# Seven chunks of the second modulation set go from TensorE's products to a running sum on VectorE

## What is computed

```python
mod = jax.nn.silu(c) @ w_ada[l] + b_ada[l]
sh1, sc1, gt1, sh2, sc2, gt2 = jnp.split(mod[:, None, :], 6, axis=-1)
h = rms_norm(x, g_pre_mix[l]) * (1.0 + sc1) + sh1
...
mix = jnp.concatenate([o_diff, o_nat], axis=-1) @ w_out[l]
x = x + gt1 * rms_norm(mix, g_post_mix[l])
h2 = rms_norm(x, g_pre_ffn[l]) * (1.0 + sc2) + sh2
f = moe_ffn(h2, ...)
x = x + gt2 * rms_norm(f, g_post_ffn[l])
```

## Time and profile before

| what | us |
|---|---|
| median of 3 runs | 1941.0 (1939.54 to 1942.81) |
| profiled execution, own time | 1943.13 |
| its span, first to last instruction | 1940.8 |
| TensorE (PE) busy | 1879.4 (97%) |
| VectorE (DVE) busy | 667.3 (34%) |
| ScalarE (ACT) busy | 370.3 (19%) |
| mean granted TensorE clock | 0.998 of 2.4 GHz |

### The profile page before, as it was taken

How to read it: one execution, slowest core, us unless ns; L and a number is a source line. 1 busy time by engine, 2 the same in 40 slices (tenths; PEclk the granted TensorE clock), 3 DMA queues, 4 the chain that set the end, 5 groups by cost and what they waited for, 6 DMA issues and landing times.

```text
span 1940.8 us, 25687 instructions
## 1 busy us (share of the span) xinstructions
PE 1879.4 (97%) x9767; PEld 1135.4 (59%) x9768; DVE 667.3 (34%) x1289; ACT 370.3 (19%) x836; POOL 35.3 (2%) x57
## 2 busy tenths in 40 slices
PE   8999999999999999999989999999999999999998
PEld 6877544333334434443333336878887489988864
DVE  2451411011011111110110113354656557655564
ACT  2232211111011111110110103442111031321111
POOL 2200000000000000000000001000000000000000
PEclk9999999999999999999999999999999999999999
DMA  9959699999989979999999999324544452345430
GB/s 370 289 209 411 253 421 422 422 422 421 422 346 400 422 302 422 421 422 422 421 422 421 422 422 320 126 87 130 172 165 167 147 164 97 109 158 162 161 116 22
DMA packets 156542, 564.45 MB, mean 291 GB/s; under 512 B 10814, under 2 KB 94040, under 8 KB 101952
## 3 DMA queue, kind: packets, MB, share of 16 engines
q1 hardware_dynamic: 153312, 554.96, 73.8%
q0 software_dynamic: 2416, 7.87, 1.3%
q10 hardware_dynamic: 752, 0.75, 0.1%
HBM read 562.49 MB, written 1.05 MB: 290 GB/s over the span
## 4 chain that ended last, share of the span: by engine, by line
PE 79%; DMA 14%; SPq 4%; DVE 1%; issue 1%; ACT 1%; ACTq 0%; DVEq 0%
PE psum L1038 15%; DMA ring<-in_w_dram 14%; PE psum L1422 12%; PE psum L1066 9%; PE psum L1514 6%; PE psum L1214 5%; SPq L581 4%; PE psum L1566 4%; PE psum L793 3%; PE psum L860 3%; PE psum L1008 2%; PE psum L1025 2%; PE psum L1450 2%; PE psum L1626 2%; PE psum L1047 1%; PE psum L1592 1%
## 5 line engine op out<-in xcount | busy, mean ns | idle before, releaser
L1038 PE MATMUL psum<-ring,arena 128*64 128x512 f32 x2176 | 491.2, 596 | 38.8 <-DMA ring<-in_w_dram 38.8
L1038 PEld LDWEIGHTS psum<-ring,arena 128*64 128x64 f32 x2176 | 151.9, 137 | 369.5 <-issue 252.0
L2496 DVE TENSOR_SCALAR arena<-psum 128x512 f32<-128x512 f32 x34 | 23.5, 692 | 726.0 <-PE psum L1047 726.0
L1066 PE MATMUL psum<-ring,arena 128*64 128x512 f32 x1088 | 241.0, 595 | 3.2
L1066 PEld LDWEIGHTS psum<-ring,arena 128*64 128x64 f32 x1088 | 77.6, 137 | 145.1 <-issue 145.1
L1856 ACT ACTIVATE arena<-arena 128x512 f32<-128x512 f32 x34 | 21.4, 630 | 558.5 <-DVE arena L2496 558.5
L1422 PE MATMUL psum<-arena,mixT 128*128 128x256 f32 x528 | 120.9, 379 | 0.0
L1422 PEld LDWEIGHTS psum<-arena,mixT 128*128 128x128 f32 x528 | 98.8, 190 | 12.6
L1422 PE MATMUL psum<-ring,hT 128*128 128x256 f32 x352 | 83.5, 379 | 0.0
L1008 PE MATMUL psum<-arena 128*128 128x128 f32 x544 | 75.1, 281 | 0.0
L1008 PEld LDWEIGHTS psum<-arena 128*128 128x128 f32 x544 | 65.9, 191 | 11.7 <-issue 11.7
(11 more groups left out here) (521 smaller groups left out, 2256.1 us busy)
## 6 DMA issues: line engine op xcount, KB each, us to landing
ring<-in_w_dram SPq DMA_DIRECT2D x384, 1024.0 KB, 23.0
ring<-in_ffn_w_dram SPq DMA_DIRECT2D x66, 1024.0 KB, 5.4
ring<-in_w_ada_dram SPq DMA_DIRECT2D x16, 1024.0 KB, 10.5
ring<-in_odd_w_in_dram SPq DMA_DIRECT2D x16, 1024.0 KB, 5.5
ring<-in_even_w_in_dram SPq DMA_DIRECT2D x13, 1024.0 KB, 12.8
ring<-in_w_in_dram SPq DMA_DIRECT2D x12, 1024.0 KB, 36.5
ring<-in_ada_blocks_dram SPq DMA_DIRECT2D x8, 1024.0 KB, 17.3
ring<-in_w_out_dram SPq DMA_DIRECT2D x4, 1024.0 KB, 14.3
```

Source lines behind the costliest of these rows:

```text
L1038: mm = nc.tensor.matmul(bank[4 + q][64 * h:64 * h + 64, :], xg[:, k, SLOTS * r:SLOTS * (r + 1)], ring[(C_MOE + k) % RING][:, (2 * h + q) * ...
L1066: mm = nc.tensor.matmul(bank[7][64 * h:64 * h + 64, :], act_T[:, at:at + 64], w[:, k, 512 * h:512 * h + 512], start=(f == 0), stop=(f == 7))
```

## The change

Chunks m = 0 to 6 of the second set are no longer multiplied by TensorE. VectorE multiplies each by silu(c) of its rows and adds it to a running sum of 128 x 2048 (`added_rows`, arena columns 0 to 2047) in slots 13 (three of them), 17, 19 (two) and 21. TensorE adds the sum over the partitions into bank 7 with four matmuls against ones in slot 24 (`added_sum`), then takes chunk 7 in slot 24, 8 to 11 in slot 25, 12 to 15 in slot 26. `chunk_done` is raised by eight with chunk 7. The third set goes to bank 1. The load of `h_tok` waits for the sum to be read (`ada_summed`). `heads(7)` and `ada_columns(0)` move into `out_first`, behind its first seven eighths.

```diff
-ADA_B_PER_SLOT = N_ADA_B // WIN_TAIL
+ADA_ADDED_AT = (13, 13, 13, 17, 19, 19, 21)
+ADDED = len(ADA_ADDED_AT)
+ADA_AT = {WIN_SLOTS: (7,), WIN_SLOTS + 1: range(8, 12), WIN_SLOTS + 2: range(12, 16)}
...
+        added_rows = region(0, 2048)
...
-            pool.wait_ge(S.mix_saved, DIFF_HEADS)
+            pool.wait_ge(S.ada_summed, 1)
             pool.dma_start(h_tok, x[0].rearrange("(a p) d -> p a d", p=P)).then_inc(S.tok_loaded, 16)
...
+            def added_sum():
+
+                pe.wait_ge(S.ada_added, ADDED)
+                for g in range(4):
+                    mm = nc.tensor.matmul(bank[7][32 * g:32 * g + 32, :], ones[:, 0:32], added_rows[:, 512 * g:512 * g + 512],
+                                          start=True, stop=False)
+                mm.then_inc(S.ada_summed, 1)
+
+            def ada(m):
+
+                home = (bank[7], bank[1])[m // KT]
+                arrived(C_ADA_B + m)
+                w = ring[(C_ADA_B + m) % RING]
+                if m == KT:
+                    pe.wait_ge(S.proj_saved, N_WIN)
+                k = m % KT
                 for g in range(4):
                     mm = nc.tensor.matmul(home[32 * g:32 * g + 32, :], silu_c[:, k, :], w[:, 512 * g:512 * g + 512],
-                                          start=(k == 0), stop=(k == KT - 1))
-                mm.then_inc(S.chunk_done, 1)
+                                          start=(m == KT), stop=(k == KT - 1))
+                mm.then_inc(S.chunk_done, ADDED + 1 if m == ADDED else 1)
...
                 if slot < WIN_SLOTS:
                     win_half(slot // 2, slot % 2)
-                else:
-                    for n in range(ADA_B_PER_SLOT):
-                        ada(N_ADA_A + ADA_B_PER_SLOT * (slot - WIN_SLOTS) + n)
+                if slot == WIN_SLOTS:
+                    added_sum()
+                for m in ADA_AT.get(slot, ()):
+                    ada(m)
                 if slot in TURN_AT:
                     turn_attention(TURN_AT.index(slot))
-                if slot in HEADS_AT:
+                if slot in HEADS_AT[:-1]:
                     heads(HEADS_AT.index(slot))
...
-            ada_columns(0)
...
                 for n, some in enumerate((range(KT - 1), (KT - 1,))):
+                    if n == 1:
+                        heads(UNITS - 1)
+                        ada_columns(0)
                     pe.wait_ge(S.mix_saved, UNITS - 1 + n)
...
-                V.tensor_copy(ada_rows[n + 1], (bank[7], bank[3])[n]).then_inc(S.ada_saved, 1)
+                V.tensor_copy(ada_rows[n + 1], (bank[7], bank[1])[n]).then_inc(S.ada_saved, 1)
...
+            def add_block(m):
+
+                n = C_ADA_B + m
+                dve.wait_ge(landed[n % RING], 16 * (n // RING + 1))
+                w, factor = ring[n % RING], silu_c[:, m, 0:1]
+                if m == 0:
+                    dve.wait_ge(S.c_ready, 1)
+                    V.tensor_scalar(added_rows, w[:, :], factor, None, ALU.mult).then_inc(S.ada_added, 1)
+                else:
+                    dve.wait_ge(S.ada_added, m)
+                    V.scalar_tensor_tensor(out=added_rows, in0=w[:, :], scalar=factor, in1=added_rows,
+                                           op0=ALU.mult, op1=ALU.add).then_inc(S.ada_added, 1)
+
...
                 if slot in SUB_SCALE_AT:
                     sub_scale(SUB_SCALE_AT.index(slot))
+                for m in range(ADDED):
+                    if ADA_ADDED_AT[m] == slot:
+                        add_block(m)
```

More of the change, by code:

```diff
@@ L276, in shape_constants @@
     return early, late
-NAMES = """ada_saved ada_turned c_loaded c_turned alibi_loaded vec_loaded x_loaded early_loaded bias_loaded lam_loaded moe_loaded late_loaded cmp_loaded
+NAMES = """ada_saved ada_turned ada_added ada_summed c_loaded c_turned alibi_loaded vec_loaded x_loaded early_loaded bias_loaded lam_loaded moe_loaded late_loaded cmp_loaded
 ident_loaded vec_turned vec_saved c_cleared c_ready x_turned x_ready lam_dots lam_spread lam_exp bias_ready
```

## The result

The changed kernel takes 1944.6 us (median of 22 runs, 1941.94 to 1950.85), the kernel before beside it on the same chips 1941.7 (22 runs). The ratio is 1.0017, 95% interval 1.0010 to 1.0025: 3.3 us slower (1.9 to 4.9), where 2.6 were forecast; the medians differ by 2.9. TensorE has less to do and the kernel takes longer.

A forecast was written before the change was run, and what follows sets the result against it. TensorE and nearly tied DMA transfers were taken as bounds; with h_tok's 2.46 in the stream, w_out lands at 157.0, plus 9.02 ends out_first at 166.0 against 163.40: 1941.0 + 2.6 = 1943.6 us, range 1940.0 to 1947.2.

The forecast's parts named there:

- main case: Modulation chunks 12 to 15 and w_out paced by transfers at full clock: 2.6 us slower, 1943.6; chance 47%.
- The transfers end last, and the saving is given back to them: Ahead of out_first's end: TensorE has 5.4 us less to do but loses it waiting for transfers; end 166.0 against 163.40.
- h_tok's megabyte costs about what its bytes take: In the ring's stream from about 140 us: the load delays every chunk from 12 on by 2.46 us, bounds 0 to 3.6.
- The rival of a load that costs little: h_tok's packets fall into holes or w_out's first chunk loses its lag: out_first ends 162.4 to 164.5, 1940.0 to 1942.1; 14%.
- TensorE's own order: From 135.96 us to out_first's end, if only TensorE's sequence limited: 159.05, 4.35 less than 163.40.
- VectorE's steps are covered: Slots 13 to 21: seven products of 2.46, 17 us in all, fit idle stretches and cost nothing; one shift 0.35 late.
- A microsecond at out_first's end is one at the end of the kernel: The expert stage begins when TensorE gets there, so a microsecond at 163.40 carries through to the kernel's end.
- The first release costs nothing, w_out lands at 154.5 without other traffic: Chunk 12's slot frees at about 137.75 instead of 136.85, covered by chunk 11's transfer; w_out's first landing stays at 154.5.
- Waits of 1 to 1.6 at each of the last four chunks: Sign in the trace after: at line 722, chunks 12 to 15 each wait 1 to 1.6 us for the ring's transfer.
- The clock's fall, 1.7 to 3.4 with a chance of 30%: Rival: TensorE's clock drops in the transfer-paced stretch and out_first loses 1.7 to 3.4 us; 1945.3 to 1947.0, chance 30%.
- 2.0 of work that could have filled the wait has been moved behind it: heads(7) and ada_columns(0), formerly done ahead of the wait for w_out, now follow it: 2.0 us.
- The rival of the saving that arrives: Up to out_first's end only TensorE's order limits: 4.35 us less, 1936.7; needs chunks landing 8 us earlier; chance 7%.

The follow-up runs named there:

- the order undone: The changed kernel with heads(7) and ada_columns(0) put back ahead of out_first's first product; 1948.89 us, ratio 1.0045.
- one filler: The changed kernel with one idle product of 512 columns on TensorE behind each of chunks 12, 13 and 14; 1944.34 us, ratio 1.0013.
- the load moved alone: The kernel before with only h_tok's load moved, to wait for the last saved projection (about 137 us); 1943.57 us, ratio 1.0006.
- early slots: The changed kernel with slots of chunks 0 to 6 released by VectorE's count and SP's loads reordered; 1938.17 us, ratio 0.9983.

## Why the prediction was right

By the prediction's own signs the number is better borne out than its main case. That case was transfers at full clock; "a granted clock below 1.00 between 146 and 164" was to be wrong, and all three profiles of the changed kernel have it. out_first was to wait 1 to 2 us for w_out, and in none of the three did it: chunk 15's product and the turn, slowed by the lower clock, ended later than w_out's landing. The time fits because the fall cost 0.8 and not 1.7 to 3.4.

**Held.** The steps below, each with what was measured.

- *The transfers end last, and the saving is given back to them.* Chunks 13 to 15 wait 2.36, 1.43 and 0.55; removing the load of h_tok leaves the length of before (27.45 and 27.73 against 27.35), not 5.4 less.
- *h_tok's megabyte costs about what its bytes take.* I took 2.46 within 0 to 3.6. w_out's first chunk landed 2.3 later with the load in the stream than without (156.4 against 154.1), and 2.6 later in the kernel before. For chunk 15 it was more. Where chunk 15 had to be waited for, its product gives the landing: in six profiles with the load in the stream it starts 18.15 to 19.51 behind the first landmark (mean 18.80; the changed kernel thrice, the order undone, one filler, the load moved alone), in the two without it 15.85 and 16.12. The difference is 2.8; in the kernel before, the load moved alone put chunk 15 back by 3.7, past my upper bound. The rival of a load that costs little rested on holes in the stream, and a common set of engines, which I held against it, does not exclude those: the full stream, 420 to 425 GB/s, left none.
- *TensorE's own order.* Paper said 159.05 if nothing else paced it; with early slots it ended at 158.99. This carries the wait for VectorE (1.0 forecast, 0.94 measured) and the 9.02 of out_first (9.12 measured with one filler, 157.15 to 166.27).
- *VectorE's steps are covered.* 15.6 us against 17 forecast, the shift 0.02 late instead of 0.35. A sum of product and chunk over 2048 columns took 2.34 to 2.35, the first, a product alone, 1.28.
- *A microsecond at out_first's end is one at the end of the kernel.* From the start of the first expert's product to the span's end lie 1734.3 to 1736.1 us in the profiles without a fall of 6.8 us behind it (the three highest of these, 1735.1 to 1736.1, have one of 3.4 us near 1210), and 1737.7 to 1739.4 in those with one or two, wherever that stage starts between 198.5 and 208.4.

**The sizes that were off, all small.**

- *The first release costs nothing, w_out lands at 154.5 without other traffic.* It landed at 154.1, but by two errors that cancelled: chunk 15 came at 151.65 instead of 150.9, and the 1.1 of lag on w_out's first chunk was gone. The first of these is the later first release, which was to cost nothing: SP issued chunk 12 at 137.83 instead of 137.02, it landed at 144.2 instead of 143.4, and the 0.8 stayed to chunk 15. Why the chunk in flight did not cover it is open, since by 145 the engines had moved only 0.07 MB less. The lag's going was luck.
- *Waits of 1 to 1.6 at each of the last four chunks.* The load shares the engines with the ring for 7 us instead of pushing it aside at once. Chunk 12 was hardly late in the profile of the result (0.67 and 1.20 of waiting in the other two), chunk 13 took the brunt (3.4 from landing to landing where 2.46 is usual), and w_out's first chunk came at 156.44 where I had 157.0.
- *The clock's fall, 1.7 to 3.4 with a chance of 30%.* The mechanism came in every profile of the changed kernel, so 30% was low, and its price was high. What the end would be at full clock I can only work out: it is chunk 15's landing plus 2.48 for w_out plus 9.12: a length of 29.76, 29.75 and 30.83 in the three profiles, against 30.98, 29.76 and 31.90. The fall cost 1.2, 0 and 1.1, mean 0.8, because most of it lay inside waits for the ring, where it is free. The page of the Trainium skill that I weighed (TensorE: Matmul & The Clock Gate, Why this matters for your kernels), with its idle gaps longer than any of mine, spoke against this rival; the trace disagrees, for the gaps here were at most 2.4 us. The measurement decides.

Put together: the mean full-clock length of the three profiles is 30.1, 2.8 above before's 27.35; with the clock's 0.8 it is 3.5 above, and the runs say 3.3 (1.9 to 4.9). The forecast of 2.6 lacked the clock's share; the interval alone could not tell the two apart.

**The step that was wrong, without a price.** "2.0 of work that could have filled the wait has been moved behind it". It could not have filled it: heads(7) needs ScalarE's copy of a turn that itself ends late, and with the old order the stretch is longer, 32.11 against 29.76 to 31.90. Chunk 15 was 0.7 later there than the mean of the six, and about 1.0 is the order's own (w_out at 157.8 and 9.12 would give 166.9 instead of 167.90).

**What I did not see.** The rival of the saving that arrives had 7%, because "no row offers room" for landings 8 us earlier. In the changed kernel that is so; but the view of the stretch 98 to 136 had shown an idle stream in front of a saturated one, and the slots that VectorE had read were the room.

## What to carry to other kernels

Work taken off an engine that is tied with the transfers is worth at most the slack between the two; before making it faster, ask which loads the edit moves, and through which wait on the place that its scratch data takes. If another engine now reads the ring, let its count hand the slots back and order the loads by when slots come free: only with that did the removed products become worth 3 us here, where without it they cost 3. And in a kernel whose clock falls at changing places, compare landmarks of several profiles, since one span is some 3.5 us off by a single fall of 6.8 us.

## What the runs showed of the hardware

- The granted clock went from 2.4 to 1.2 GHz in the paced stretch in four of four profiles that had the seven chunks removed, the load of h_tok in the stream and no filler in the waits (2.4 us the longest of them), in the first of them after 3.42 us with 1.06 of work. In the kernel before with the load moved alone, whose one wait is 1.21, it stayed at 1.00. So it did without the load, with waits of 1.4 and 4.68 of 8.00 us busy:

```profile
146.00:154.00 8.00, 4.68 (x40) 1.33 (x32) 2.70 (x4) 1.91 (x8) 0.00 (x0) 1.00 1.01 424
```

That is the kernel with h_tok's load late; with one filler TensorE was busy 8.40 of 10.50 and the clock stayed too. What decides between them was not tried.

- The clock also fell for 6.8 us with TensorE busy throughout, at 223.4 in the kernel before, at 227.9 with the order undone, at 226.4 and again at 1216.2 with one filler, at 1214 and 1218 in two of the three profiles of the changed kernel, and at neither place in the third. One of them:

```profile
1214.00:1220.80 6.80, 6.80 (x74) 6.22 (x74) 0.00 (x0) 2.62 (x5) 0.00 (x0) 0.50 0.67 228
```

From the first expert's product to the span's end it is 1734.6 on average in the four profiles without any such fall, 1735.4 in the three with one of 3.4 us, 1738.2 in the four with one of 6.8 us and 1739.4 in the one with two: a fall of 6.8 us costs some 3.5. How much of the scatter from run to run this is was not measured.

- Two full queues did not share the engines' time evenly: 35% for GpSimd's, 65% for SP's. By packets they did, 268 against 274; GpSimd's carried 3.9 KB on average (1.04 MB) and SP's 7.3 (1.99 MB). The window of the profile with the order undone has 261 against 262. The same megabyte that landed after 8.9 us in an almost empty stream took 11.1.
